# A decoder layer on one core: the last two pieces of the last down projection in another order, and the last norm bank by bank

## Reference

```
def rms_norm(x, g):
    y = xf * lax.rsqrt(jnp.mean(xf * xf, axis=-1, keepdims=True) + NORM_EPS)
    return (y * g)

x = x + 0.5 * rms_norm(swiglu_1(rms_norm(x, ..)), ffn1_post_g)
x = x + rms_norm(mix(rms_norm(x, ..)), mix_post_g)
h = (silu(x' @ w_gate) * (x' @ w_up)) @ w_down      # x' = rms_norm(x, ffn2_pre_g), FFN_DIM = 5632
x = x + 0.5 * rms_norm(h, ffn2_post_g)
```

## Time and profile before

| | |
|---|---|
| time, median of 3 runs | 1879.92 us (1879.79 to 1879.96) |
| profiled execution, span | 1880.0 us |
| TensorE busy | 1854.7 us, 99% of the span |
| VectorE busy | 935.5 us, 50% |
| ScalarE busy | 799.3 us, 43% |
| GpSimd busy | 27.6 us, 1% |
| mean granted clock of TensorE | 0.997 |

### The profile page before, as it was taken

One profiled execution on the slowest core, in us unless ns is written; L12 is line 12 of the kernel. 1 busy time (PEld: TensorE's weight loads), 2 busy tenths in 40 slices (PEclk: granted clock), 3 DMA queues, 4 the chain that ended last, 5 costly groups with the idle time before them and its releaser, 6 DMA issues.

```text
span 1880.0 us, 21535 instructions
## 1 busy us (share of the span) xinstructions
PE 1854.7 (99%) x8239; PEld 1499.2 (80%) x8239; DVE 935.5 (50%) x853; ACT 799.3 (43%) x791; POOL 27.6 (1%) x59
## 2 busy tenths in 40 slices
PE   8999999999999999999999999999999999999997
PEld 6888888888878888788887878888888888788886
DVE  5444444444454555665567464444444444455545
ACT  6333433344344444543346445334333343444443
POOL 0000000000000000000000000000000000000000
PEclk9999999999999999999999999999999999999999
DMA  9545554555555545364441554455555555555452
GB/s 361 183 178 184 190 184 178 181 186 189 180 179 187 193 180 194 131 222 179 162 151 49 183 195 179 179 181 186 190 179 180 184 190 182 179 181 195 183 184 106
DMA packets 49063, 341.09 MB, mean 181 GB/s; under 512 B 5438, under 2 KB 5764, under 8 KB 9092
## 3 DMA queue, kind: packets, MB, share of 16 engines
q1 hardware_dynamic: 48944, 340.58, 50.4%
q10 hardware_dynamic: 84, 0.04, 0.0%
HBM read 338.50 MB, written 2.10 MB: 181 GB/s over the span
## 4 chain that ended last, share of the span: by engine, by line
PE 97%; DVE 1%; ACT 1%; issue 0%; DMA 0%; DVEq 0%; POOL 0%; ACTq 0%
PE banks L1188 25%; PE banks L1095 23%; PE banks L1093 23%; PE banks L1094 22%; PE banks L1158 1%; PE banks L1110 1%; PE banks L1318 0%; PE banks L1317 0%; DVE rows L735 0%; PE banks L1327 0%; DMA raw<-in_weights 0%; ACT w_hi L478 0%; PE banks L1337 0%; DVE scaled L786 0%; PE banks L1338 0%
## 5 line engine op out<-in xcount | busy, mean ns | idle before, releaser
L702 DVE TENSOR_TENSOR w_lo<-raw,w_hi 128x2048 fp32r<-128x2048 f32 (+3 forms) x229 | 515.3, 2250 | 672.2 <-ACT w_hi L395 672.0
L395 ACT ACTIVATE w_hi<-raw 128x2048 fp32r<-128x2048 f32 (+3 forms) x229 | 431.0, 1882 | 759.6 <-PE banks L1095 754.9
L1093 PE MATMUL banks<-w_hi,act_hi 128*128 128x512 f32 (+1 forms) x1728 | 687.6, 398 | 3.7 <-DVE act_lo L711 2.8
L1095 PE MATMUL banks<-w_hi,act_lo 128*128 128x512 f32 (+1 forms) x1728 | 684.1, 396 | 0.0
L1094 PE MATMUL banks<-w_lo,act_hi 128*128 128x512 f32 (+1 forms) x1728 | 680.0, 394 | 0.0
L1093 PEld LDWEIGHTS banks<-w_hi,act_hi 128*128 128x128 f32 x1728 | 326.0, 189 | 77.6 <-issue 3.2
L1095 PEld LDWEIGHTS banks<-w_hi,act_lo 128*128 128x128 f32 x1728 | 325.7, 188 | 77.8
L1094 PEld LDWEIGHTS banks<-w_lo,act_hi 128*128 128x128 f32 x1728 | 326.0, 189 | 76.5
L1188 PE MATMUL banks<-w_hi,hid_split 128*128 128x512 f32 x1408 | 385.6, 395 | 0.0
L775 DVE TENSOR_TENSOR w_lo<-raw,w_hi 128x2048 fp32r<-128x2048 f32 x88 | 201.7, 2292 | 236.1 <-ACT w_hi L478 236.1
L1188 PEld LDWEIGHTS banks<-w_hi,hid_split 128*128 128x128 f32 x1408 | 264.2, 188 | 64.0 <-DVE hid_split L778 0.5
(11 more groups left out here) (119 smaller groups left out, 613.5 us busy)
## 6 DMA issues: line engine op xcount, KB each, us to landing
raw<-in_weights SPq DMA_DIRECT2D x307, 1024.0 KB, 4.8
raw<-in_weights SPq DMA_DIRECT2D x6, 512.0 KB, 3.9
gain_row<-in_post_gains SPq DMA_DIRECT2D x3, 1024.0 KB, 6.9
raw<-in_weights SPq DMA_DIRECT2D x4, 768.0 KB, 4.2
raw<-in_weights SPq DMA_DIRECT2D x4, 640.0 KB, 3.9
xT<-in_x_turned SPq DMA_DIRECT2D x4, 512.0 KB, 10.3
rows<-in_x SPq DMA_DIRECT2D x2, 1024.0 KB, 13.8
out_rows<-rows SPq DMA_DIRECT2D x8, 256.0 KB, 2.7
```

Of the source, the lines that this page charges most:

```text
L395: nc.scalar.activation(w_hi[:, pc.split, 0:width], raw[:, pc.slot, 0:width], ACT.Copy)\
L702: nc.vector.tensor_tensor(w_lo[:, pc.split, 0:width], raw[:, pc.slot, 0:width], w_hi[:, pc.split, 0:width], ALU.subtract).then_inc(lo_read ...
L1093: nc.tensor.matmul(out_ap, hi, rhs_hi, start=start, stop=False, skip_group_check=chain)
L1095: return nc.tensor.matmul(out_ap, lo, rhs_hi, start=False, stop=stop, skip_group_check=chain)
```

## The change

TensorE takes pieces A and B together. It goes tile by tile and bank by bank: for tile 0 and its first bank the 6 matmuls of A, then the 6 of B; then the same for its second bank; then for tile 1. That is the same 48 matmuls, each group of 12 closed with a semaphore `last_bank_done`. The wait for B's `lo_ready` stands ahead of B's first 6. The loop over the pieces of this half does four rounds instead of five; two more pieces ahead of A are written out.

ScalarE squares one bank at a time, four instructions of 128 x 512. VectorE, in `finish`, takes over the sum for `var` (a tensor_scalar on 128 x 1) and scales one bank at a time; GpSimd does only the power. The adds and stores are as before.

```diff
 # scalar
+            def square_last():
+                for t in range(TILES):
+                    for n in range(2):
+                        act.wait_ge(last_bank_done, 2 * t + n + 1)
+                        square(banks[:, down_banks(1, t) + n, :], junk[:, 0:BANK], t, 1 + n)
 # gpsimd
-            inverse_rms(R_POST2, 2, D, 0.5)
+            inverse_rms(R_POST2, 1, D, 0.5)
+            for t in range(TILES):
+                pool.wait_ge(last_var_ready, 2 * t + 2)
+                nc.gpsimd.tensor_tensor(rs[:, R_POST2, t:t + 1], var[:, R_POST2, t:t + 1],
+                                        minus_half[:, t:t + 1], ALU.pow).then_inc(last_rs_ready, 1)
 # vector
+            def finish():
+                def add_part(t, n):
+                    dve.wait_ge(squared, LAST_SUMS + 2 * t + n + 1)
+                    if n:
+                        dve.wait_ge(last_var_ready, 2 * t + 1)
+                    nc.vector.tensor_scalar(var[:, R_POST2, t:t + 1], sumsq[:, t, 1 + n:2 + n], 4.0 / D,
+                                            var[:, R_POST2, t:t + 1], ALU.mult, ALU.add).then_inc(last_var_ready, 1)
+                    nc.vector.tensor_tensor(scaled[:, t, quarter(2 + n)], banks[:, down_banks(1, t) + n, :],
+                                            gain_row[:, quarter(2 + n)], ALU.mult).then_inc(y_scaled, 1)
...
+                for t in range(TILES):
+                    for n in range(2):
+                        add_part(t, n)
+                    dve.wait_ge(last_rs_ready, t + 1)
+                    dve.wait_ge(y_scaled, 8 + 2 * OUT_BLOCKS + 2 * t)
+                    for k in range(4):
+                        add(t, k)
 # tensor
+                    with pe.Fori(0, (HALF - 6) // 4) as i:
+                        for n in range(2, 6):
+                            down_piece(piece(stage + HALF + n, i, 4), 1)
+                    for n in range(4, 2, -1):
+                        down_piece(piece(PIECES - n), 1)
+                    last_pieces(piece(PIECES - 2), piece(PIECES - 1))
+            def last_pieces(*pair):
...
+                for t in range(TILES):
+                    for n in range(2):
+                        for pc in pair:
+                            if t == 0 and n == 0:
+                                pe.wait_ge(lo_ready, pc.index + 1)
+                            mm = passes(pc, t, n)
+                        mm.then_inc(last_bank_done, 1)
```

More of the change, by code:

```diff
@@ L86 @@
 G_ROWS = 4 * DC + QC + KVC
+VAR_STEPS, LAST_SUMS = 2 * (1 + 2 + 1 + 1 + 1 + 1 + 1 + OUT_BLOCKS + 1 + 1), 28
 MOBA_TAB, MLA_TAB = 3 * HD // 2, 3 * ROPE // 2
@@ L224, in build_layer @@
         y_scaled = sem("y_scaled")
+        last_bank_done = sem("last_bank_done")
+        last_var_ready = sem("last_var_ready")
+        last_rs_ready = sem("last_rs_ready")
         scores_ready = sem("scores_ready")
@@ L372, in inverse_rms @@
                                                          var[:, job, one], ALU.mult, ALU.add))
-                        if n == parts - 1:
+                        if n == parts - 1 and job != R_POST2:
                             nc.gpsimd.tensor_tensor(rs[:, job, one], var[:, job, one], minus_half[:, one], ALU.pow)\
@@ L694, in _ @@
             down(GU2, DOWN2)
-            square_down(DOWN2, 1)
+            square_last()
         @block.vector
@@ L737, in add @@
                         in1=rows[:, t, quarter(k)], op0=ALU.mult, op1=ALU.add).then_inc(rows_ready, 1)
[L739 to L743, removed]
                 for k in range(4):
@@ L754, in add_residual, with add @@
                 turn_low(turn, 3)
-            scaled_parts = {R_POST1: 4, R_POST_MIX: 4 + 2 * OUT_BLOCKS, R_POST2: 8 + 2 * OUT_BLOCKS}
+            scaled_parts = {R_POST1: 4, R_POST_MIX: 4 + 2 * OUT_BLOCKS}
+            def finish():
[7 more added lines that the diff above has]
+                                            gain_row[:, quarter(2 + n)], ALU.mult).then_inc(y_scaled, 1)
+                def add(t, k):
+                    nc.vector.scalar_tensor_tensor(
+                        out=rows[:, t, quarter(k)], in0=scaled[:, t, quarter(k)], scalar=rs[:, R_POST2, t:t + 1],
+                        in1=rows[:, t, quarter(k)], op0=ALU.mult, op1=ALU.add).then_inc(rows_ready, 1)
+                dve.wait_ge(var_ready, VAR_STEPS)
+                for t in range(TILES):
[5 more added lines that the diff above has]
+                        add(t, k)
             def gate_up(stage):
@@ L1085, in _ @@
             down(GU2, DOWN2, 26, 3)
-            add_residual(R_POST2, None, lambda t: scale_down(1, 28, t))
+            finish()
         @block.tensor
@@ L1203, in down, with passes @@
                     down_piece(piece(stage + HALF + n), 1, n == 0)
-                with pe.Fori(0, (HALF - 2) // 4) as i:
-                    for n in range(2, 6):
-                        down_piece(piece(stage + HALF + n, i, 4), 1)
+                if stage == DOWN1:
+                    with pe.Fori(0, (HALF - 2) // 4) as i:
+                        for n in range(2, 6):
+                            down_piece(piece(stage + HALF + n, i, 4), 1)
+                else:
+                    with pe.Fori(0, (HALF - 6) // 4) as i:
+                        for n in range(2, 6):
+                            down_piece(piece(stage + HALF + n, i, 4), 1)
+                    for n in range(4, 2, -1):
+                        down_piece(piece(PIECES - n), 1)
+                    last_pieces(piece(PIECES - 2), piece(PIECES - 1))
+            def last_pieces(*pair):
+                def passes(pc, t, n):
+                    rhs_hi, rhs_lo = cut(w_hi, pc.split, 2, D // 2), cut(w_lo, pc.split, 2, D // 2)
+                    for j in range(2):
+                        hi = hid_split[:, pc.split, 0, j, tile_of(t)]
+                        lo = hid_split[:, pc.split, 1, j, tile_of(t)]
+                        for lhs, rhs in ((hi, rhs_hi), (hi, rhs_lo), (lo, rhs_hi)):
+                            mm = nc.tensor.matmul(banks[:, down_banks(1, t) + n, :], lhs, rhs[:, j, quarter(n)],
+                                                  start=False, stop=True, skip_group_check=True)
+                    return mm
+                for t in range(TILES):
[5 more added lines that the diff above has]
+                        mm.then_inc(last_bank_done, 1)
             def turn_latent(first, chunks, bank, col, count):
```

## The result

| | before | changed |
|---|---|---|
| median | 1880.07 us (1879.06 to 1882.17, 16 runs) | 1884.97 us (1882.70 to 1885.91, 16 runs) |
| profiled span | 1880.0 us | 1881.2 us |
| mean clock of the profiled execution | 0.997 | 0.998 |

The ratio is 1.002 (95% interval 1.0013 to 1.0027): slower by 2.4 to 5.1 us, at the edge of what the measurement tells. The medians lie 4.9 us apart, the means of the same runs 4.0. The forecast was 1883.0 with a range to 1884.9 and +3.1 us; the median lies 0.07 us above the range and nearer to the rival with the long low clock (1884.5) than to the forecast.

The account below looks back on a forecast made before the run. TensorE's matmul stream was taken as the bound, busy 99% of the span. +3.8 (stall) +1.4 (clock) -2.0 (tail) = +3.1 gave 1883.1 us, 1883.0 against the median; range 1881.3 to 1884.9.

Parts of the forecast that it names:

- the rival with the long low clock: Behind the new TensorE gap the low clock lasts twice as long, 2.9 us in place of 1.4: 1884.5; chance 0.18.
- The wait: TensorE waits for B behind 6 matmuls of A instead of 24 and resumes at 1864.15, 3.78 us late.
- The clock: After the new gap TensorE's clock falls for some 3.3 us, slowing 7 matmuls: 1.4 us, bounds 0 and 2.9.
- the thin stretch at 1113 us: TensorE nearly idle from 1113.37 to 1115.91, then clock 0.51 until 1119.4; taken as evidence for the new gap.
- the prediction's own last line: Prediction wrong if idle is below 3 us, low clock missing or twice, or tile 1's adds over 2 us late.
- The tail: From TensorE's last matmul to the end: 7.6 us in place of 9.66, 2.0 us given back.
- The unknown small sum: VectorE's sum for `var` in the tail, absent from the trace; taken as 0.17 us from a 128 x 2 tensor_scalar.
- 1.1 forecast: VectorE finishes scaling tile 1's first bank and is free 1.1 us before tile 1's last small sum.
- The matmuls' order and the code: 12 matmuls in a row to one bank and written-out pieces cost nothing; up to 1 us as the code's bound.
- The base: The profiled execution of the kernel before the change was taken to lie 0.08 us over the median.

Follow-up runs that it names:

- e5_wait12: Changed kernel with 12 matmuls of A, not 6, ahead of the wait for B; median 1881.89 us against 1881.04 before the change, ratio 1.0004.
- e4_wait18: Changed kernel with 18 matmuls of A, not 6, ahead of the wait for B; median 1880.54 us against 1881.27 before the change, ratio 0.9997.
- e2_third: Changed kernel with a third buffer for piece A, so B is ready before A begins; median 1878.62 us against 1881.27 before the change, ratio 0.9988.
- e1_fill: Changed kernel with 15 unused matmuls filling TensorE's wait for B; median 1882.73 us against 1881.27 before the change, ratio 1.0008.
- e9_look: Changed kernel unaltered, profiled once more; one run, +4.5 us over before the change from A's first matmul to the end.
- e7_pool_sum: Changed kernel with its small sum back on GpSimd; one run, +3.3 us over before the change from A's first matmul to the end.

## Why the prediction was right, and where it was off

*The wait.* Right in size and place: 3.8 us forecast; by the rows TensorE resumes at 1862.09 where the stream would have gone on at 1858.17 + 0.23, 3.7 us later. e5_wait12 and e4_wait18 shorten the gap by 1.4 us each; e2_third, without it, is 5.2 us faster than the changed kernel from A's first matmul on.

*The clock.* The mechanism was right and the size for a single low stretch too (1.4 forecast, 1.36 by e1_fill). The evidence for it was weaker than I took it for: the low clock behind the thin stretch at 1113 us is missing in five of 13 profiles, so that row didn't promise one behind the new gap. Behind the new gap it came in all five profiles. What was off is how often it lasts twice as long: I gave this 0.18, and by the prediction's own last line ("or comes twice") e9_look speaks against it. One profile in five shows it, and of the timed spans of the changed kernel 7 of 16 and 4 of 11 lie at 1883.4 to 1884.1 with a mean clock of 0.995, which none of the 60 timed runs of before on the experiments' chips shows (0.996 to 0.998). That those runs all are of the kind of e9_look is inferred from their clock, not shown one by one. It would put the mean cost at 3.1 + 1.4 x 0.4 = 3.7 us, beside the 3.6 and 3.8 that the medians on one chip and the first ratio give. But the intervals of both ratios take in 3.1 as well, so the timed runs alone don't show that the mean lies above the forecast.

The Trainium skill ("TensorE: Matmul & The Clock Gate", "HAM oscillation — how this bites in real kernels") lets a group of matmuls behind a long wait begin at the lower clock. The traces agree for the gap of 3.5 us, with 0.50 in all five profiles. Behind shorter waits they show both: 0.50 behind the 2.1 us of e5_wait12, 1.00 behind the 0.7 us of e4_wait18, and now one, now the other behind the thin stretch at 1113 us.

*The tail.* Forecast 7.6 us with the adds 1.65 behind the last matmul; measured 7.6 and 1.66. The unknown small sum took 0.21 us, not 0.17. VectorE was idle for 1.19 us ahead of it, 1.1 forecast.

*The matmuls' order and the code.* Nothing, as taken: e2_third's 48 matmuls fill 11.2 us without a gap.

*The base.* The 0.08 us between profile and median compared a span with a time that holds 1.8 us more. It did no harm, because the +3.1 was worked out within one profile and the 0.08 only took the sum back to the median of the runs.

## What to carry to other kernels

Before a consumer is reordered to finish one output early, ask when each of its inputs is ready: here the second input had 0.56 us of slack, and the order that shortened the tail by 2.0 us asked for it 4.2 us earlier. A gap on TensorE costs its own length and can cost more at the lower clock behind it (1.3 to 2.8 us here behind 3.7 us, nothing behind 0.7 us); if the wait can't go, work that keeps TensorE busy takes that part away, and a third buffer takes away all of it. Where executions differ by more than the effect, compare from a landmark just ahead of the change to the end, in several profiles.

## What the runs showed of the hardware

- Behind a gap of 3.7 us on TensorE the granted clock was 0.50 for 3.4 us in four profiles and for 6.8 us in one, with the same program. Behind 2.1 us it fell in the one profile taken (e5_wait12), and by the timed runs probably not in every execution; behind 0.7 us it did not fall in the one profile of e4_wait18.
- The low stretch at 1116 us, upstream of the change, appears in some executions of one kernel and not in others (three of the five profiles of the changed kernel); over all kernels those without it reach A at 1856.9 to 1857.4, those with it at 1858.2 to 1859.2.
- A sum of one number per partition on GpSimd took 0.27 us beside VectorE's scale (e7_pool_sum, three times) and 0.93 and 1.25 us beside VectorE's adds (e7_pool_sum and before).
